# Where the split weights and the moving tiles of a three-block kernel start, modulo 256 bytes

## The reference

```
# both later layers
qkv = xn @ w_qkv                      # 2048 x 6144, layer one
k, v = xn @ w_kv ; q = xn @ w_q       # 2048 x 4096 and 2048 x 2048, layer two
x = x + o @ w_o                       # 2048 x 2048, each layer
up = xn @ w_up                        # 2048 x 11264, each layer
x = x + (silu(conv(g)) * u) @ w_down  # 5632 x 2048, each layer
```

## Time and profile before

| | |
|---|---|
| Time, median of 3 runs (lowest to highest) | 2731.57 us (2731.21 to 2732.09) |
| Profiled execution: span from first to last instruction | 2730.8 us; of its time around the span nothing is given |
| Mean granted TensorE clock | 0.999 |
| Busy share | PE 100%, PEld 87%, DVE 73%, ACT 44% |
| HBM | 523.8 MB read, 193 GB/s |

### The profile page before, as it was taken

One profiled execution on the slowest core, in us unless ns is written; L12 is line 12 of the kernel. 1 busy time (PEld: TensorE's weight loads), 2 busy tenths in 40 slices (PEclk: granted clock), 3 DMA queues, 4 the chain that ended last, 5 costly groups with the idle time before them and its releaser, 6 DMA issues.

```text
span 2730.8 us, 44046 instructions
## 1 busy us (share of the span) xinstructions
PE 2717.8 (100%) x15292; PEld 2370.7 (87%) x15292; DVE 1981.4 (73%) x2594; ACT 1198.5 (44%) x1533; POOL 5.7 (0%) x12
## 2 busy tenths in 40 slices
PE   9999999999999999999999999999999999999999
PEld 7888888888888888888888888888888888888888
DVE  6647577777777777657777666698877775677765
ACT  2003454455554444444444443366444444444443
POOL 0000000000000000000000000000000000000000
PEclk9999999999999999999999999999999999999999
DMA  9996655555556666566666566644666665666664
GB/s 335 353 284 199 202 185 192 166 167 164 157 164 190 189 191 190 185 192 185 191 191 182 193 192 189 185 156 128 199 184 187 187 190 192 188 191 190 185 200 146
DMA packets 705761, 528.14 MB, mean 193 GB/s; under 512 B 32205, under 2 KB 694543, under 8 KB 705423
## 3 DMA queue, kind: packets, MB, share of 16 engines
q1 hardware_dynamic: 701728, 523.60, 62.7%
q10 hardware_dynamic: 3951, 3.44, 0.4%
HBM read 523.80 MB, written 2.10 MB: 193 GB/s over the span
## 4 chain that ended last, share of the span: by engine, by line
PE 96%; DVE 2%; DMA 2%; ACT 0%; issue 0%; SPq 0%; DVEq 0%; ACTq 0%
PE acc L684 81%; PE acc L800 3%; PE acc L994 2%; PE acc L788 1%; PE sums L800 1%; PE turned L800 1%; DMA aring<-in_w_ada 1%; PE mixed L915 1%; PE sums L1132 1%; DVE pro_ada L1851 1%; PE scores L1125 0%; DVE wr L1776 0%; PE sums L700 0%; DMA w<-in_w_in 0%; PE mixed L916 0%; PE sums L871 0%
## 5 line engine op out<-in xcount | busy, mean ns | idle before, releaser
L684 PE MATMUL acc<-xs,wr 128*128 128x512 f32 (+1 forms) x7680 | 1352.0, 337 | 0.2 <-DVE wr L1776 0.2
L684 PEld LDWEIGHTS acc<-xs,wr 128*128 128x128 f32 x7680 | 1174.4, 188 | 163.7 <-issue 3.8
L1776 DVE TENSOR_TENSOR wr<-raw,wr 128x1024 fp32r<-128x1024 f32 x832 | 1000.9, 1222 | 348.2 <-ACT wr L1308 336.5
L1308 ACT ACTIVATE wr<-raw 128x1024 fp32r<-128x1024 f32 x832 | 871.4, 1058 | 732.5 <-PE acc L684 721.1
L684 PE MATMUL acc<-ys,wr 128*128 128x512 f32 (+1 forms) x4352 | 760.9, 336 | 0.7 <-DVE wr L1776 0.6
L684 PEld LDWEIGHTS acc<-ys,wr 128*128 128x128 f32 x4352 | 664.8, 188 | 91.3 <-DVE wr L1776 1.2
L684 PE MATMUL acc<-wr,xs 128*128 128x512 f32 (+1 forms) x1024 | 183.3, 337 | 0.0
L684 PEld LDWEIGHTS acc<-wr,xs 128*128 128x128 f32 x1024 | 157.0, 188 | 23.0 <-issue 0.5
L1660 ACT ACTIVATE ffn_cv<-ffn_cv 128x256 f32<-128x256 f32 x88 | 36.9, 419 | 245.4 <-DVE ffn_cv L2383 245.4
L1787 DVE TENSOR_REDUCE ffn_ug<-acc 128x512 f32<-128x1024 f32 x88 | 107.7, 1224 | 39.6 <-PE acc L684 39.6
L1851 DVE SCALAR_TENSOR_TENSOR pro_ada<-aring,small,pro_ada 128x512 f32<-128x512 f32 (+1 forms) x103 | 85.7, 833 | 33.2 <-DMA aring<-in_w_ada 27.4
(11 more groups left out here) (324 smaller groups left out, 1484.7 us busy)
## 6 DMA issues: line engine op xcount, KB each, us to landing
raw<-in_ffn_w_up SPq DMA_DIRECT2D x704, 256.0 KB
raw<-in_ffn_w_down SPq DMA_DIRECT2D x160, 512.0 KB
raw<-in_a_w_qkv SPq DMA_DIRECT2D x96, 512.0 KB
raw<-in_b_w_kv SPq DMA_DIRECT2D x64, 512.0 KB
aring<-in_w_ada SPq DMA_DIRECT2D x96, 256.0 KB, 7.2
w<-in_w_in SPq DMA_DIRECT2D x48, 512.0 KB
raw<-in_w_ada SPq DMA_DIRECT2D x32, 512.0 KB, 5.0
raw<-in_w_out SPq DMA_DIRECT2D x32, 512.0 KB
```

What stands on the lines that cost most here:

```text
L684: mm = pe.matmul(*ops, start=first and ops is wide, stop=last and ops is wide)
L1308: f(wr[:, s, :, 0:256], raw[:, s, :].rearrange("p (k n) -> p k n", k=UK), ACT.Copy)\
L1776: tt(wr[:, s, :, 256:512], raw[:, s, :].rearrange("p (k n) -> p k n", k=UK), wr[:, s, :, 0:256], ALU.subtract).then_inc(T.unit_split[s].se ...
```

## The change

The ring `wr` becomes two parts, each for two slots. A part holds the high halves of its two slots in one run of 8192 bytes and the low halves in another; the second run starts `HALF_PAIR` = 2·4·256 + 52 elements (8400 bytes) after the first. With a shift of 4 elements from an address of 0 modulo 256, the high run starts at 16 and the low run at 224 modulo 256. `xs` and `ys` lie in tensors that are 32 bytes longer and start 16 bytes into them, at 80 modulo 256. ACT and DVE write a unit's half as one run of 1024 elements instead of four of 256. In a `tokens_out` product the 512 moving columns of the weights are now two runs of 256 columns (`both_halves`). The number and the order of the instructions, the waits and the loads are as they were. The first block's `w1` is now at 0 modulo 256, `xm` stays at 64, and tensors behind `wr` move by the sizes and gaps.

```diff
-WEIGHTS_STEP, MOVING_STEP = 160, 64
+WEIGHTS_STEP, TILES_STEP, MOVING_SHIFT = 0, 64, 16
+HALF_PAIR = 2 * UK * 256 + 52
+WEIGHTS_SHIFT = 4
+SLOT_PAIR = -(-2 * HALF_PAIR // 64) * 64
...
-        wr = sb("wr", [RING, UK, 512], F32R)
-        w1 = nc.alloc_sbuf_tensor_at("w1", [P, ONE_SPACE], F32, offset=wr_at)
+        wr = sb("wr", [2, SLOT_PAIR], F32R)
+        w1 = nc.alloc_sbuf_tensor_at("w1", [P, ONE_SPACE], F32, offset=-(-wr_at // 32) * 32)
...
-        xs = sb("xs", [KT, 2 * TOK], F32R)
-        xs_at = nc.sbuf_base - KT * 2 * TOK * 4
+        stream = sb("stream", [KT * 2 * TOK + 2 * MOVING_SHIFT // 4], F32R)
+        xs_at = nc.sbuf_base - KT * 2 * TOK * 4 - 2 * MOVING_SHIFT
+        def moving_tiles(tensor, tiles):
+            return tensor[:, MOVING_SHIFT // 4:MOVING_SHIFT // 4 + tiles * 2 * TOK].rearrange("p (k n) -> p k n", k=tiles)
+        xs = moving_tiles(stream, KT)
...
+        def slot_of(s):
+            return wr[:, s // 2, WEIGHTS_SHIFT:WEIGHTS_SHIFT + 2 * HALF_PAIR].rearrange("p (h n) -> p h n", h=2)[:, :, s % 2 * UK * 256:(s % 2 + 1) * UK * 256]
+        def half_of(part, s):
+            return slot_of(s)[:, part, :]
...
-                    w, x, first, last = wr[:, s, k - k0, :], right(k), k == 0, k == blocks - 1
+                    both_halves = slot_of(s)[:, :, (k - k0) * 256:(k - k0 + 1) * 256]
+                    high, low = both_halves[:, 0, :], both_halves[:, 1, :]
...
                         if tokens_out:
-                            wide = (a[:, j, :], x[:, cols], w)
-                            short = (a[:, j, 0:256], x[:, low], w[:, 0:256])
+                            wide = (a[:, j, :], x[:, cols], both_halves)
+                            short = (a[:, j, 0:256], x[:, 256 + j * P:256 + j * P + P], high)
                         else:
-                            wide = (a[:, j, :], w[:, cols], x)
-                            short = (a[:, j, 0:256], w[:, low], x[:, 0:TOK])
+                            wide = (a[:, j, :], high[:, cols], x)
+                            short = (a[:, j, 0:256], low[:, cols], x[:, 0:TOK])
...
-                    f(wr[:, s, :, 0:256], raw[:, s, :].rearrange("p (k n) -> p k n", k=UK), ACT.Copy)\
+                    f(half_of(0, s), raw[:, s, :], ACT.Copy)\
...
-                    tt(wr[:, s, :, 256:512], raw[:, s, :].rearrange("p (k n) -> p k n", k=UK), wr[:, s, :, 0:256],
-                       ALU.subtract).then_inc(T.unit_split[s].sem, 1)
+                    tt(half_of(1, s), raw[:, s, :], half_of(0, s), ALU.subtract).then_inc(T.unit_split[s].sem, 1)
```

More of the change, by code:

```diff
@@ L350, in program @@
         ARENA = 32 * 1024
[L351 to L354, removed]
-        xs = sb("xs", [KT, 2 * TOK], F32R)
-        xs_at = nc.sbuf_base - KT * 2 * TOK * 4
+        begin_at("slab_gap", TILES_STEP)
+        SLAB = YS + 2 * MOVING_SHIFT + ARENA
+        slab = ctx.enter_context(nc.sbuf_tensor("slab", [P, SLAB], mybir.dt.uint8))
+        base = nc.sbuf_base - SLAB
+        begin_at("stream_gap", TILES_STEP)
+        stream = sb("stream", [KT * 2 * TOK + 2 * MOVING_SHIFT // 4], F32R)
[3 more added lines that the diff above has]
+        xs = moving_tiles(stream, KT)
         xm = nc.alloc_sbuf_tensor_at("xm", [P, KT, TOK], F32, offset=xs_at)
@@ L359, in program @@
         gate_sum = nc.alloc_sbuf_tensor_at("gate_sum", [P, GATE_COLS], F32, offset=xs_at + KT * TOK * 4)
-        ys = nc.alloc_sbuf_tensor_at("ys", [P, GROUP, 2 * TOK], F32R, offset=base)
+        ys = moving_tiles(nc.alloc_sbuf_tensor_at("ys", [P, GROUP * 2 * TOK + 2 * MOVING_SHIFT // 4], F32R, offset=base), GROUP)
         class Overlay:
@@ L368, in __call__ @@
                 self.at += -(-n * int(np.prod(shape)) // 32) * 32
-                assert self.at <= base + YS + ARENA, (self.prefix, name, self.at - base)
+                assert self.at <= base + SLAB, (self.prefix, name, self.at - base)
                 return nc.alloc_sbuf_tensor_at(self.prefix + name, [P, *shape], dt, offset=where)
-        tail = base + 16 * 2 * TOK * 4
+        tail = base + 16 * 2 * TOK * 4 + 2 * MOVING_SHIFT
         aring = nc.alloc_sbuf_tensor_at("aring", [P, ADA_RING, 1024], F32, offset=base)
@@ L405, in program @@
         kB, vB = o("k", [B_HEADS, TOK]), o("v", [2, B_HEADS * HD])
-        o = Overlay("ffn_", base + YS)
+        o = Overlay("ffn_", base + YS + 2 * MOVING_SHIFT)
         UG = [o(f"ug{e}", [2, 2 + TOK]) for e in range(2)]
@@ L672, in unit_product @@
                         before(k)
-                    w, x, first, last = wr[:, s, k - k0, :], right(k), k == 0, k == blocks - 1
+                    both_halves = slot_of(s)[:, :, (k - k0) * 256:(k - k0 + 1) * 256]
+                    high, low = both_halves[:, 0, :], both_halves[:, 1, :]
+                    x, first, last = right(k), k == 0, k == blocks - 1
                     for j in range(2):
                         cols = slice(j * P, j * P + P)
-                        low = slice(256 + j * P, 256 + j * P + P)
                         if tokens_out:
-                            wide = (a[:, j, :], x[:, cols], w)
-                            short = (a[:, j, 0:256], x[:, low], w[:, 0:256])
-                        else:
-                            wide = (a[:, j, :], w[:, cols], x)
-                            short = (a[:, j, 0:256], w[:, low], x[:, 0:TOK])
+                            wide = (a[:, j, :], x[:, cols], both_halves)
+                            short = (a[:, j, 0:256], x[:, 256 + j * P:256 + j * P + P], high)
+                        else:
+                            wide = (a[:, j, :], high[:, cols], x)
+                            short = (a[:, j, 0:256], low[:, cols], x[:, 0:TOK])
                         for ops in ((short, wide) if last else (wide, short)):
```

## The result

The changed kernel takes 2694.81 us (median of 4 runs, 2694.43 to 2696.17) against 2731.59 us before: a ratio of 0.9865, 95% interval 0.9853 to 0.9877. The profiled execution has a span of 2692.5 us, 38.3 us less than before, with the same 15292 matmuls at the full clock.

A forecast was written before the change was run, and what follows sets the result against it. The number of matmuls times the time from one to the next bounds the kernel. Gains of 24.7 + 2.1 = 26.8 us off the 2730.8 us span give 2704.0, plus 0.8 for the median: 2704.8 us, range 2652 to 2757.

The forecast's parts named there:

- What bounds the kernel: TensorE busy 2717.8 of 2730.8 us; number of matmuls times the time from one to the next sets the end.
- The placement with features out: 6016 features-out pairs of line 684: 346.9 to 342.8 ns a pair, 24.7 us gained.
- The reason for the sign: Features-out pairs: a gain, because 21 ns lay down to the float32 rows and 4 ns up to the dearest row.
- my bound: Features-out pair without the extra, by the float32 rows: 325.9 ns, 126 us gained at most.
- Distance: Stationary start less moving start modulo 256 at line 684: 96 costs 13.4 ns extra a matmul, 160 costs 15.5.
- slower: Rival, chance 0.27: distances 144 and 192 are dear, features-out pairs go to 351.0 ns, 2754 us.
- Tokens out: 512 tokens-out pairs: 351.0 to 346.9 ns, 2.1 us gained, nothing taken for the jump between the runs.
- The splits: ACT's and DVE's writes in one run, 832 each, 1058 and 1222 ns: no effect on the time taken.
- The first block: Its 1750 matmuls, nearly all plain float32, with `w1` moved: nothing taken, at most 4.6 us gained or lost.
- Nothing moves: Rival, chance 0.12: the extra is inside TensorE wherever operands lie; pair stays 346.9 ns, time 2731.6 us.
- the rule cited there: Trainium skill on SBUF: TensorE has its own ports and waits for no one; weight loads read by an independent port.
- The conflict goes away almost whole: Rival, chance 0.11: two distances chosen apart remove most of the pair's extra; 2634 us, or about 2593 with all.

The follow-up runs named there:

- the layout alone: Changed kernel's new layout (halves in runs, one write each, two-run tokens-out operand) at the old placement, 160, 160, 64: 2732.14 us against 2732.05 before, ratio 1.000.

## Why the prediction was right

Faster was forecast, 2704.8 us in a range of 2652 to 2757, and 2694.8 measured.

**What bounds the kernel** was right: the pairs of line 684 set the end, nothing else became late, and the gain is spread evenly over them.

**The placement with features out** was the step that was mis-sized: I took one step of 4.1 ns a pair (24.7 us) and it was 6.28 ns (37.8 us). The step was read from the one pair of streams that the trace had to offer; the levels are 816, 824, 832, 840 and 848 cycles, and the change moved the pair by two of them, 832 to 816, where I took a little more than one.

**The reason for the sign does not stand.** I argued from room: 21 ns down to the float32 rows, 4 ns up. The room below isn't there (no placement of 1024 with features out is under 340.0 ns, 14 ns above my bound), and upwards there is more (363 ns in steps of 16 bytes, 377 in steps of 4). With the moving tiles at 80, 167 of 256 cells are dearer than 834 cycles and 11 cheaper than 830: from that argument alone a draw would more likely have lost. The sign came out right because the change sits on one of the few cheap cells, and nothing in the trace of before could tell that: the direction was luck.

**Distance** was right as a variable and incomplete: the moving start modulo 32 belongs to it, and at some placements the state that a stream is in. The rival "slower" read nearness between distances as likeness; the table shows that 96 and 112 lie 16 cycles apart. Still, its price is real: the kernel moved back by 16 bytes has the distances 192 and 144, the rival's 351.0 ns with features out, 347.0 for its 346.9 with tokens out, and 2752 us for its 2754. Between the result and that rival stood 16 bytes on all operands.

**Tokens out**: I took the pair at the cost of distance 96, 346.9 ns, and it came to 349.9, a gain of 0.6 us and not 2.1. Two runs with two distances aren't the mean of the two; the jump between the runs by itself costs nothing, as the layout alone at the old placement showed (81.43 us, the same as before).

**The splits** were right at nothing: 1058 and 1222 ns stand unchanged. **The first block**, taken at nothing too, keeps its 215.9 ns and ends 1.3 us earlier, inside the 4.6 us it was allowed. In the layout alone, with `w1` at 160 as before, it ends 0.6 us earlier, so whether the rest is the address is not shown.

**Nothing moves** is refuted, and with it what was drawn from the rule cited there, that no placement could matter: in the sweeps in steps of 16 bytes the stream takes up to 23 ns a pair more (871.9 against 816 cycles) by the addresses of two operands that TensorE alone reads. What in TensorE does this is not shown. The rule may hold between engines: nothing here gives a sign that DVE, ACT or DMA change the pair, since sweeps without them have the kernel's 816 and 832 cycles.

**The conflict goes away almost whole** was wrong about the floor, which is 340.0 ns and not 325.9. The changed kernel is 0.6 ns above that floor: a product ends with a wide matmul and the next begins with one, and there the trace has 233 ns from one to the next instead of 227, with two or three slower steps behind it.

## What to carry to other kernels

Where TensorE streams float32r back to back, compare the time from matmul to matmul with columns / 2.4 GHz; what is over is worth a sweep of start addresses in steps of 16 bytes, stationary against moving operand, in a kernel of its own that does nothing else. A few hundred placements fit into one run of 1.7 ms, the cheap ones are few (5 in 256) and have dear neighbours, so measure the very placement and don't interpolate. Then look at every long stretch of the real kernel, since one placement can have two steady states, and try a placement behind more than one predecessor.

## What the runs showed of the hardware that was not expected

- The cost of a float32r pair comes in levels 8 cycles apart, 816 to 848 for most placements (518 of the 768 streams with features out in steps of 16 bytes lie within a cycle of a multiple of 8); it goes with stationary less moving start modulo 256 and the moving start modulo 32, and at some placements with the state that a stream is in. At the placements tried it did not change with 1024- or 2048-byte strides (346.9 ns with either) or with the other engines idle (340.0 against 340.6 ns).
- Moving all operands together by 32 bytes changes nothing (2695.2 us), by 16 bytes 57 us (2752.3 us).
- The extra does not shrink with the columns of the weight load (416 cycles a matmul with 128, 96 and 64 columns at the old placement); with 96 columns all four placements tried have 416.
- One placement had two steady states in one execution, 347.8 and 362.7 ns a pair, with a change of state inside one product after a step 64 ns late.
- bfloat16 takes its columns and 6 cycles at both placements tried; float32r with 128 moving columns takes 268 cycles at all sixteen.
- Open: what in TensorE's reading makes the levels, why the lowest has 32 cycles over the columns with 512 and 384 of them and 16 with 256, and which start leads to which of two states.
